# Scores as one float32 matmul each, a fused row maximum, a transposed copy of x as an input, and a new placement of the steps

## The chip, the core and the metric

The program runs on one core of one Trainium2 chip. The metric is the device time of one execution in microseconds (us). The core has five engines that run side by side, each with its own instruction queue in program order: TensorE (PE in the profile, its weight loads PEld), VectorE (DVE), ScalarE (ACT), GpSimd (POOL) and SyncE (SP), which issues nearly all DMAs. They meet through semaphores.

## What is computed

Two identical decoder layers (own weights) over 256 tokens of width 1024, all in float32:

```
xn = RMSNorm(x);  h = xn @ W_in            # 2956 columns for the four mixers
A: stick-breaking attention, strictly causal: z = q.k*scale, log-sigmoids, reverse cumulative sum, exp, @ v
B: softmax(q1 k1) - lambda * softmax(q2 k2), causal, heads of 2 x 32, RMSNorm of q, k and of the output
C: causal softmax attention (block-sparse; with 256 tokens every row sees its own block alone)
D: gated sum of three branches: 15 compressed keys; selected keys; window keys (own K and V each)
merged = sum_i sigmoid(xn @ Wg_i + b_i) * (o_i @ Wb_i)
x = x + merged @ W_out
x = x + (silu(y @ W1) * (y @ W3)) @ W2     # y = RMSNorm(x), hidden width 2816
```

There are 4 heads of 64; the tolerance calls for float32-like results.

## The kernel before, in words

**Weights by chunks.** All weights of a layer are cut into `NCH` chunks (list `CHUNKS`): each is 256 rows by up to 512 columns, 512 KB. For chunk `n` SP loads `w_raw` (a ring of 4), ACT rounds it into `w_hi` (L874, type fp32r, which PE takes in one pass), DVE puts the rest into `w_lo` (L1092), and PE (`products`, L609) makes 12 products of 512 columns: hi x hi, hi x lo and lo x hi, for two row tiles and two row blocks. ACT and DVE work `LEAD` = 2 chunks ahead of PE. The activations that meet the weights are split into hi and lo in the same way (`xt`, `ot`, `ht`).

**Steps between the chunks.** Everything else is a list of small steps. The table `PLAN` gives each step the chunk number `u` ahead of which it stands, and `RANK` its order within one `u`; every engine walks through the same lists and does its own part of each step. ACT and DVE do steps of rank under 3 before their split of chunk `u + 2`, the others after it. PE does all steps of `u` first and then the 12 products of `u`. Below, "at 38" means ahead of chunk 38. Steps that matter here:

- `x0` to `x3` (`pair`, L665): four transposes of x by PE into the PSUM tile `att`, then hi (ACT, L894) and lo (DVE, L1102).
- `Aq`, `Ak`, ... `Dk` (`qk`, L688): transposes of queries and keys. ACT copies them to `qk_hi` (L910), DVE makes `qk_lo` (L1180, L1183).
- `z` and `sm` (`causal`, L702): the scores of a pair of heads (or of the two maps of B): for each causal half of the rows hi x hi, hi x lo, lo x hi, each for both heads, which lie on different rows of PE (64 rows each, 32 in B) and go to the banks S0 and S1. `A` has 2 such steps a layer, B 4, C 2, D 4: 24 in the program, 12 matmuls each.
- DVE's part of `sm` (L1231) adds the mask and takes the row maximum; L1236 scales and negates it; ACT makes the exponentials (L930); DVE's `p` (L1248 to L1253, L1257 to L1265) scales them. `pt` (L743) transposes them in 3 pieces, ACT copies these to `ptb` (L996), and `pv` (L768; L759 in B) multiplies with v. L768 is true float32: its two halves lie on different columns of PE.
- `kct`, `cs`, `cp`, `cpt`, `cpv`: the compressed branch of D. `cs` (L839, L841) makes its scores in 16 small matmuls into S0 and S1, and DVE adds mask and low part from there (L1303, L1307).
- `o0` to `o3`: the outputs of the mixers into `ot`; `o1` is transposed by PE (L665 from `osb`).

A step that writes a bank of `att` waits for the last reader of that bank (`bank_free`): TP for transposes, S0 and S1 for scores, OB for `pv`.

Of the kernel before, what the change touches and what calls it, by code (L numbers as in the profile page):

```python
# [7 lines left out]
ALU = mybir.AluOpType  # L8
# [57 lines left out]
WARM_UP = 6, 7  # L66
RAW, WR, LEAD = 4, 4, 2


def in_cols(g):  # L70
# [9 lines left out]
    "stats": 3, "lambda": 18, "x": (0, 0, 1, 2), "f": (-2, -1, 1, 2), "m": (-1, -1, 2, 3), "h": 6,  # L80
    "sig": (50, 54, 56, 58), "o": (20, 43, 43, 58), "subln": 35, "prep": (13, 19, 27), "ngate": 27, "Aq": 6,
    "Ak": 7, "Az": (8, 14), "Asp": (11, 16), "Acum": (13, 19), "Apv": (14, 20), "Bq": 19, "Bk": 20,
    "Bsm": (21, 24, 27, 28), "Bp": (21, 24, 27, 29), "Bpt": (23, 27, 29, 32), "Bpv": (27, 29, 31, 33), "Bo": 33,
# [3 lines left out]
    "Dpt": (42, 43, 44, 45, 50, 51, 52, 54), "Dpv": (45, 53, 53, 55),  # L87
# [23 lines left out]
def maps_of(mixer, n):  # L111
# [11 lines left out]
    "x0": 0, "f0": 0, "m0": 0, "proj": 3, "zg": 4.5, "merge": 0.5, "xadd": 2.5, "act": 5, "Acum": 3.5, "Dp": 2,  # L123
    "cpv": 4, "sig": 3, "Cpv": 0.5, "cbuild": 1.5, "kct": 0.5, "x": 0.5, "Asp": 6, "Bpv": 3.5, "ck": 0.5,
    "cv": 4.5, "cs": 3.5, "prep": 1, "Csm": 4, "Dpv": 1, "lambda": 1, "stats": 1, "subln": 4.5, "Bsm": 4.5,
    "Bpt": 5.5, "ngate": 2, "Cp": 6, "h": 3, "kcprep": 1.5, "f": 4, "Bp": 4.5,
# [68 lines left out]
def steps_at(l, u):  # L195


    early = [("pair", ("x", kp)) for kp in range(2)]
    if u == NCH:
        return [(l, s) for s in STEPS[u]] if l == DEPTH - 1 else []  # L200
    todo = [(l, s) for s in STEPS[u] if not (l and s in early)]
# [14 lines left out]
class Events:  # L216


    def __init__(self, sem, order):
        self.sem, self.order, self.count = sem, order, 0  # L220
        self.place = {k: n for n, k in enumerate(order)}

    def at(self, layer, key):

        return layer * len(self.order) + self.place[key] + 1
# [71 lines left out]
def trunk_kernel(nc, x, w_in, w_gate, w_branch, w_out, w_ffn_gate, w_ffn_up, w_ffn_down,  # L297
                 norm_g, gains, lam, cmp_pe, cmp_w, b_gate, const, masks, out):
    with ExitStack() as ctx:
# [6 lines left out]
        def place(name, shape, dt, at=None):  # L306
# [20 lines left out]
        end_big = top[0]  # L327
        squares = place("squares", [P, NT, NC], F32, at=zg_at)
# [15 lines left out]
        qk_hi = [place(f"qk_hi{i}", [P, 4, SEQ], F32R) for i in range(2)]  # L344
        qk_lo = [place(f"qk_lo{i}", [P, 4, SEQ], F32R, at=zg_at + 4 * D_MODEL * (4 * i + 3)) for i in range(2)]
        kc_hl = place("kc_hl", [P, 2, 16], F32R)
# [37 lines left out]
        stat = [sm(104 + 4 * i, 4) for i in range(2)]  # L384
# [25 lines left out]
        s_ident = sem("identity_landed")  # L410
# [4 lines left out]
        s_x = [sem(f"x_quarter_landed{kp}") for kp in range(KT // 2)]  # L415
# [16 lines left out]
        att_done = Events(sem("att_done"), att_keys)  # L432
# [3 lines left out]
        hi_done = Events(sem("hi_done"), [s for s in keys("pair", "qk", "kct") if s[1] != "Dc"])  # L436
# [5 lines left out]
            "lambda", "prep", "ngate", "kcprep", "subln", "cbuild", "sm", "p", "sp", "cp")])  # L442
# [58 lines left out]
        def _(sp):  # L501
# [8 lines left out]
            def load_x(kp):  # L510
                cols = slice(2 * kp * P, (2 * kp + 2) * P)
                sp.dma_start(xs[:, :, cols], x[0, :, cols].rearrange("(t p) d -> p t d", p=P)).then_inc(s_x[kp], 16)


            load_x(0)
            sp.dma_start(ident, const[:, C_ID:C_ID + P]).then_inc(s_ident, 16)
            for k, landed in enumerate((s_half, s_raw[0])):
                sp.dma_start(w_raw[:, 0, k, :], w_in[0, k * P:(k + 1) * P, 0:NC]).then_inc(landed, 16)
            load_x(1)
            load_chunk(1)  # L520
            load_x(2)
            load_chunk(2)
            load_x(3)
# [43 lines left out]
        def _(pe):  # L567
# [10 lines left out]
            def products(l, u):  # L578
# [33 lines left out]
                if n < DEPTH * NCH - 1:  # L612
# [10 lines left out]
                    if n == 0:  # L623
                        pair(0, ("pair", ("x", 1)))
# [15 lines left out]
            def pair(l, step):  # L640
# [3 lines left out]
                if what == "x":  # L644
                    if l:
                        pe.wait_ge(dve_acc.sem, dve_acc.at(l - 1, ("xadd", ("down", kp // 2))))
                    else:
                        pe.wait_ge(s_ident, 16)
                        pe.wait_ge(s_x[kp], 16)
# [18 lines left out]
            def qk(l, step):  # L668
# [3 lines left out]
                if name[0] == "A":  # L672
                    pe.wait_ge(proj_out.sem, proj_out.at(l, ("proj", 0)))
                elif name == "Dc":
# [16 lines left out]
            def causal(buf, maps, swap=False):  # L691
# [5 lines left out]
                at = 0  # L697
                for t, (c0, c1) in enumerate((first, second)):
                    for a_, b_ in ((qk_hi, qk_hi), (qk_hi, qk_lo), (qk_lo, qk_hi)):
                        for i, (r, q, k) in enumerate(maps):  # L700
                            still, move = (k, q) if swap else (q, k)
                            mm = pe.matmul(att[:, S0 + i, at:at + c1 - c0], a_[buf][r, still, t * P:(t + 1) * P],  # L702
                                           b_[buf][r, move, c0:c1], start=not swap and t == 0 and a_ is b_,
                                           stop=t == 1 and a_ is qk_lo,
                                           skip_group_check=True)
                    at += c1 - c0
                return mm

            def scores(l, step):
# [3 lines left out]
                if n == 0:  # L713
                    pe.wait_ge(read_dve.sem, read_dve.at(l, ("qk", mixer + "k")))
# [77 lines left out]
            warm_up(WARM_UP[0])  # L792
            for l in range(DEPTH):
                for u in range(NCH):
                    for ll, step in steps_at(l, u):
                        kind, a = step
                        if kind == "pair":
                            if own_transpose(step) and (ll or step != ("pair", ("x", 1))):
                                pair(ll, step)
                            if step == ("pair", ("x", 0)) and ll == 0:  # L800
                                warm_up(WARM_UP[1])
# [29 lines left out]
                        elif kind == "cs":  # L831
                            bank_free(l, step)
                            pe.wait_ge(read_dve.sem, read_dve.at(l, ("kct", None)))
# [691 lines left out]
```

## Time and profile before

| | before |
|---|---|
| three runs, median (lowest to highest) | 870.63 us (869.18 to 871.32) |
| the profiled execution, own time | 872.5 us |
| its span, first to last instruction | 870.6 us |
| PE, DVE, ACT, POOL busy in it | 858.9, 550.9, 469.0, 159.0 us |
| granted clock of PE, mean | 0.996 |

The profile is one execution. Its own time lies 1.9 us above the span. In its rows, "start, us, engine line, out<-in" stand for groups of like instructions; a matmul's length includes its pipeline, so the time that PE spends on one is read from start to next start. The rows used are in the section after the next.

### The profile page before, as it was taken

The numbers are of one execution on the slowest core, as the hardware profiler recorded it, in microseconds if no ns is written. First come the engines' busy times: TensorE is split into PE (matmuls) and PEld (weight loads), VectorE is DVE, ScalarE is ACT, GpSimd is POOL, SyncE is SP. The second block draws the span as 40 slices with busy tenths as digits, with TensorE's granted clock in tenths as the row PEclk, the third lists the DMA queues.
The fourth block names the chain that finished last, engine by engine and source line by source line (L and its number), as shares of the span: only waits on it lengthen the run. The fifth ranks groups of instructions, "written<-read, shape, count | busy, mean of one in ns | idle before, by whom it ended". The sixth has DMA issues, their size and how long they took to land.

```text
span 870.6 us, 11639 instructions
## 1 busy us (share of the span) xinstructions
PE 858.9 (99%) x4371; PEld 700.5 (80%) x4371; DVE 550.9 (63%) x862; ACT 469.0 (54%) x721; POOL 159.0 (18%) x165
## 2 busy tenths in 40 slices
PE   8999999999999999999999999999999999999998
PEld 6888887788888888888888888777788888888886
DVE  6557877657966555555555678766588655555552
ACT  6676654556455444543457775456654744445431
POOL 0076652002500000000000858500043000000000
PEclk9999999999999999999999999999999999999999
DMA  8745453454557655555576454543545566655552
GB/s 299 242 136 184 150 195 122 145 169 146 178 161 240 178 186 180 184 192 173 172 225 209 144 174 164 185 135 110 176 162 193 175 201 184 190 180 184 194 193 73
DMA packets 103751, 154.17 MB, mean 177 GB/s; under 512 B 6800, under 2 KB 55440, under 8 KB 103440
## 3 DMA queue, kind: packets, MB, share of 16 engines
q1 hardware_dynamic: 103552, 153.42, 54.6%
q8 instruction: 35, 0.57, 0.3%
q14 instruction: 20, 0.16, 0.1%
q10 hardware_dynamic: 144, 0.01, 0.0%
HBM read 152.35 MB, written 1.05 MB: 176 GB/s over the span
## 4 chain that ended last, share of the span: by engine, by line
PE 96%; DVE 1%; ACT 1%; DMA 1%; issue 0%; SPq 0%; ACTq 0%
PE acc L609 86%; PE att L702 2%; PE att L665 2%; PE att L743 1%; PE att L768 1%; PE att L688 1%; ACT eb L930 1%; PE att L759 1%; DMA w_raw<-in_w_in 1%; DVE eb L1231 1%; PE att L727 0%; ACT ptb L996 0%; PE att L781 0%; ACT w_hi L874 0%; DVE eb L1253 0%
## 5 line engine op out<-in xcount | busy, mean ns | idle before, releaser
L1092 DVE TENSOR_TENSOR w_lo<-w_raw,w_hi 128x1024 fp32r<-128x1024 f32 (+1 forms) x276 | 342.4, 1250 | 154.5 <-ACT w_hi L874 150.1
L874 ACT ACTIVATE w_hi<-w_raw 128x1024 fp32r<-128x1024 f32 (+1 forms) x275 | 286.6, 1050 | 127.9 <-PE acc L609 123.7
L609 PE MATMUL acc<-w_hi,xt_hi 128*128 128x512 f32 (+1 forms) x864 | 243.0, 403 | 1.0 <-ACT w_hi L871 0.8
L609 PE MATMUL acc<-w_hi,xt_lo 128*128 128x512 f32 (+1 forms) x864 | 232.2, 391 | 0.0
L609 PE MATMUL acc<-w_lo,xt_hi 128*128 128x512 f32 (+1 forms) x864 | 230.3, 388 | 0.0
L609 PEld LDWEIGHTS acc<-w_hi,xt_lo 128*128 128x128 f32 x864 | 163.1, 189 | 35.2 <-DVE xt_lo L1102 0.5
L609 PEld LDWEIGHTS acc<-w_lo,xt_hi 128*128 128x128 f32 x864 | 162.4, 188 | 33.4
L609 PEld LDWEIGHTS acc<-w_hi,xt_hi 128*128 128x128 f32 x864 | 154.7, 189 | 30.3 <-ACT w_hi L871 1.2
L1357 POOL TENSOR_SCALAR small<-small 128x2 f32<-128x2 f32 (+4 forms) x14 | 7.5, 535 | 367.7 <-ACT sq_dump L968 264.2
L930 ACT ACTIVATE eb<-eb,small 128x128 f32<-128x128 f32 x80 | 35.5, 444 | 49.6 <-DVE small L1236 49.6
L1450 POOL TENSOR_TENSOR merged<-merged,prod 128x1024 f32<-128x1024 f32 x10 | 32.4, 3241 | 159.1 <-DVE prod L1141 158.3
L609 PE MATMUL acc<-w_hi,ht_hi 128*128 128x512 f32 x176 | 47.9, 391 | 0.0
L609 PE MATMUL acc<-w_hi,ht_lo 128*128 128x512 f32 x176 | 47.6, 389 | 0.0
L609 PE MATMUL acc<-w_lo,ht_hi 128*128 128x512 f32 x176 | 47.5, 389 | 0.0
L609 PEld LDWEIGHTS acc<-w_hi,ht_lo 128*128 128x128 f32 x176 | 33.0, 188 | 6.9
L609 PEld LDWEIGHTS acc<-w_lo,ht_hi 128*128 128x128 f32 x176 | 33.0, 188 | 6.9
L896 ACT ACTIVATE ht_hi<-att 128x512 fp32r<-128x512 f32 x22 | 13.2, 599 | 46.2 <-PE att L665 46.2
L609 PEld LDWEIGHTS acc<-w_hi,ht_hi 128*128 128x128 f32 x176 | 32.7, 188 | 6.6
L955 ACT ACTIVATE silu<-acc,small 128x256 f32<-128x256 f32 x44 | 18.5, 471 | 33.2 <-PE acc L609 33.2
L1169 DVE SCALAR_TENSOR_TENSOR hid<-acc,small,silu 128x256 f32<-128x256 f32 x44 | 19.3, 479 | 27.0 <-ACT silu L955 27.0
L1106 DVE TENSOR_TENSOR ht_lo<-att,ht_hi 128x512 fp32r<-128x512 f32 x22 | 15.2, 692 | 32.4 <-ACT ht_hi L896 32.4
L1231 DVE CUSTOM_DVE_ANT_0 eb<-att,cst 128x128 f32<-128x128 f32 x80 | 23.8, 353 | 12.1 <-PE att L702 11.8
(174 smaller groups left out, 774.1 us busy)
## 6 DMA issues: line engine op xcount, KB each, us to landing
w_raw<-in_w_gate SPq DMA_DIRECT2D x64, 512.0 KB, 3.6
w_raw<-in_w_ffn_gate SPq DMA_DIRECT2D x88, 256.0 KB, 2.9
w_raw<-in_w_ffn_up SPq DMA_DIRECT2D x88, 256.0 KB, 3.2
w_raw<-in_w_ffn_down SPq DMA_DIRECT2D x44, 512.0 KB, 3.5
w_raw<-in_w_in SPq DMA_DIRECT2D x39, 512.0 KB, 4.5
w_raw<-in_w_branch SPq DMA_DIRECT2D x16, 512.0 KB, 4.0
w_raw<-in_w_out SPq DMA_DIRECT2D x16, 512.0 KB, 3.5
bg<-in_b_gate SPq DMA_DIRECT2D x8, 512.0 KB, 5.3
```

Of the source, the lines that this page charges most:

```text
L609: return pe.matmul(acc[bank0 + t][:, 0:N], x_part[:, k0 + k, t * P:(t + 1) * P], w_part[:, k, 0:N], start=first, stop=last)
L665: mm = pe.transpose(att[:, b, (2 * k + t) * P:(2 * k + t + 1) * P], src, ident)
L702: mm = pe.matmul(att[:, S0 + i, at:at + c1 - c0], a_[buf][r, still, t * P:(t + 1) * P], b_[buf][r, move, c0:c1], start=not swap and t == 0 ...
L874: act.activation(w_hi[:, n % WR, :, 0:N], w_raw[:, n % RAW, :, 0:N], copy).then_inc(s_hi, 1)
L896: ins = act.activation(dst[:, 2 * kp:2 * kp + 2, :].rearrange("p k t -> p (k t)"), att[:, b, :], copy)
L930: ins = act.activation(eb[:, e, cols], eb[:, e, cols], ACT.Exp, scale=scale, bias=nbias[r][:, j:j + 1], accum_out=sums[r][:, j:j + 1])
L955: ins = act.activation(silu[:, t, :], acc[bank_pair(l, step) + t][:, 0:FC], ACT.Silu, scale=xr["f"][:, t:t + 1])
L1092: dve.tensor_tensor(w_lo[:, n % WR, :, 0:N], w_raw[:, n % RAW, :, 0:N], w_hi[:, n % WR, :, 0:N].bitcast(F32), ALU.subtract).then_inc(s_lo, 1)
L1106: ins = dve.tensor_tensor(lo[:, 2 * kp:2 * kp + 2, :].rearrange("p k t -> p (k t)"), att[:, b, :], hi[:, 2 * kp:2 * kp + 2, :].rearrange(" ...
L1169: ins = dve.scalar_tensor_tensor(out=hid[:, a % 2, t, :], in0=acc[bank_pair(l, step) + t][:, FC:2 * FC], scalar=xr["f"][:, t:t + 1], in1=s ...
L1231: ins = dve.tensor_tensor_reduce(out=eb[:, e, cols], in0=att[:, S0 + i, cols], in1=causal_add[:, P - t * P:], scale=1.0, scalar=NEG, op0=A ...
L1450: pool.tensor_tensor(merged[:, :, cols], merged[:, :, cols], prod[:, :, half_], ALU.add).then_inc(pool_done.now(step), 1)
```

## The change

- Scores: `qk_hi` and `qk_lo` become one float32 tile `qkt`, and each score block is 4 float32 matmuls instead of 12 of type fp32r. DVE's `qk` step goes, and so does its half of `kct`. The 256-column half now comes first in all mixers. `cs` becomes 8 float32 matmuls, and DVE adds no low part.
- Row maximum: L1231 now also multiplies by minus the scale and takes the minimum, straight into `nbias`; L1236 goes. In B's `p` the reciprocal that the next operation needs is issued first.
- The host also passes x transposed (`x_t`). In layer 0 the four `x` steps read it from SBUF (`xt_raw`) without PE. `xs` is loaded later, in two halves, and the constants in one DMA one chunk earlier; half of the first weight chunk is issued by ACT's queue.
- `PLAN` and `RANK` have new numbers throughout.

```diff
-WARM_UP = 6, 7
+WARM_UP = 12
...
-    "Ak": 7, "Az": (8, 14), "Asp": (11, 16), "Acum": (13, 19), "Apv": (14, 20), "Bq": 19, "Bk": 20,
+    "Ak": 7, "Az": (9, 14), "Asp": (9, 14), "Acum": (13, 17), "Apv": (16, 22), "Bq": 19, "Bk": 20,
...
-    by_dve = kind in ("pair", "sm", "cs", "cv", "cr", "kct") or (kind == "qk" and a != "Dc") or kind == "o"
+    by_dve = kind in ("pair", "sm", "cs", "cv", "cr", "o")
...
+            def load_xt(kp):
+                sp.dma_start(xt_raw[:, 2 * kp:2 * kp + 2, :], x_t[:, 2 * kp:2 * kp + 2, :]).then_inc(s_xt[kp], 16)
+            load_xt(0)
+            sp.dma_start(w_raw[:, 0, 1, :], w_in[0, P:2 * P, 0:NC]).then_inc(s_raw[0], 16)
+            load_xt(1)
             load_chunk(1)
...
-                    if u == 5 and l == 0:
-                        sp.dma_start(cst[:, C_ID + P:], const[:, C_ID + P:]).then_inc(s_const, 16)
+                    if u in (3, 4) and l == 0:
+                        c, cols = u - 3, slice((u - 3) * NC, (u - 2) * NC)
+                        sp.dma_start(xs[:, :, cols], x[0, :, cols].rearrange("(t p) d -> p t d", p=P)
+                                     ).then_inc(s_x[c], 16)
+                    if u == 4 and l == 0:
+                        sp.dma_start(cst[:, :], const).then_inc(s_const, 16)
...
-                    if n == 0:
-                        pair(0, ("pair", ("x", 1)))
...
-                at = 0
-                for t, (c0, c1) in enumerate((first, second)):
-                    for a_, b_ in ((qk_hi, qk_hi), (qk_hi, qk_lo), (qk_lo, qk_hi)):
-                        for i, (r, q, k) in enumerate(maps):
-                            still, move = (k, q) if swap else (q, k)
-                            mm = pe.matmul(att[:, S0 + i, at:at + c1 - c0], a_[buf][r, still, t * P:(t + 1) * P],
-                                           b_[buf][r, move, c0:c1], start=not swap and t == 0 and a_ is b_,
...
+                areas = ((0, first, 0), (1, second, 2 * P)) if swap else ((1, second, P), (0, first, 0))
+                for n, (t, (c0, c1), at) in enumerate(areas):
+                    for i, (r, q, k) in enumerate(maps):
+                        still, move = (k, q) if swap else (q, k)
+                        mm = pe.matmul(att[:, S0 + i, at:at + c1 - c0], qkt[buf][r, still, t * P:(t + 1) * P],
+                                       qkt[buf][r, move, c0:c1], start=not swap and n == 0, stop=n == 1,
...
-                                    pe.matmul(att[:, S0 + h % 2, at:at + 32], qk_hi[1][q],
-                                              kc_hl[r, :, :], start=True, stop=False)
-                                    mm = pe.matmul(att[:, S0 + h % 2, at:at + 16], qk_lo[1][q],
-                                                   kc_hl[r, 0, :], start=False, stop=True)
+                                    mm = pe.matmul(att[:, S0 + h % 2, at:at + 16], qkt[1][q], kct[r, :],
+                                                   start=True, stop=True)
...
+                        part = att[:, b, k * SEQ:(k + 1) * SEQ] if l or what == "f" else xt_raw[:, 2 * kp + k, :]
+                        ins = act.activation(dst[:, 2 * kp + k, :], part, copy, scale=g)
...
+            act.dma_start(w_raw[:, 0, 0, :], w_in[0, 0:P, 0:NC]).then_inc(s_half, 16)
...
-                                                           in1=causal_add[:, P - t * P:], scale=1.0, scalar=NEG, op0=ALU.add,
-                                                           op1=ALU.max, accum_out=stat[r][:, j:j + 1])
+                                                           in1=causal_add[:, P - t * P:], scale=-(DD if mixer == "B" else HD) ** -0.5,
+                                                           scalar=-NEG, op0=ALU.add, op1=ALU.min,
+                                                           accum_out=nbias[r][:, j:j + 1])
                     ins.then_inc(read_dve.now(step), 1)
-                    dve.wait_ge(read_dve.sem, read_dve.at(l, step))
-                    dve.tensor_scalar(nbias[r][:, :], stat[r][:, :],
```

**Three places on PE where steps moved.** The rows are PE's program; each run of three `acc` rows is one chunk. First, the compressed branch: before, the end of `cs` (at 38) with C's second score block (`qk_71` and `qk_73` are A's and C's tiles) right behind it, in the same banks.

```order
L839 MATMUL att<-kc_hl,qk_hi_72 128x32
L841 MATMUL att<-kc_hl,qk_lo_74 128x16
L702 MATMUL att<-qk_hi_71 128x128 x2
L702 MATMUL att<-qk_lo_73,qk_hi_71 128x128 x2
L702 MATMUL att<-qk_hi_71,qk_lo_73 128x128 x2
L702 MATMUL att<-qk_hi_71 128x256 x2
L702 MATMUL att<-qk_lo_73,qk_hi_71 128x256 x2
L702 MATMUL att<-qk_hi_71,qk_lo_73 128x256 x2
```

After, PE from `Dk` at 38 on: `cs` (at 39, 8 matmuls) is followed by a transpose of C's probabilities, which uses bank TP.

```order
L690 MATMUL att<-cst,kdup 128x128 x4
L615 MATMUL acc<-w_hi,xt_hi 128x512 x4
L615 MATMUL acc<-w_hi,xt_lo 128x512 x4
L615 MATMUL acc<-w_lo,xt_hi 128x512 x4
L836 MATMUL att<-kct,qkt_73 128x16 x8
L742 MATMUL att<-cst,eb 128x128 x3
```

C's second score block has moved to 36, two chunks and more ahead of `cs`. Second, the first softmax of B: before, PE between B's first score block (at 21) and the transpose of its probabilities (at 23).

```order
L702 MATMUL att<-qk_hi_72,qk_lo_74 128x256 x2
L609 MATMUL acc<-w_hi,xt_hi 128x396 x4
L609 MATMUL acc<-w_hi,xt_lo 128x396 x4
L609 MATMUL acc<-w_lo,xt_hi 128x396 x4
L609 MATMUL acc<-w_hi,xt_hi 128x396 x4
L609 MATMUL acc<-w_hi,xt_lo 128x396 x4
L609 MATMUL acc<-w_lo,xt_hi 128x396 x4
L743 MATMUL att<-cst,eb 128x128 x3
```

After, the same stretch of PE:

```order
L703 MATMUL att<-qkt_73 128x256 x2
L703 MATMUL att<-qkt_73 128x128 x2
L615 MATMUL acc<-w_hi,xt_hi 128x396 x4
L615 MATMUL acc<-w_hi,xt_lo 128x396 x4
L615 MATMUL acc<-w_lo,xt_hi 128x396 x4
L767 MATMUL att<-ptb,proj 64x256 x2
L767 MATMUL att<-ptb,proj 64x128 x2
L615 MATMUL acc<-w_hi,xt_hi 128x396 x4
L615 MATMUL acc<-w_hi,xt_lo 128x396 x4
L615 MATMUL acc<-w_lo,xt_hi 128x396 x4
L742 MATMUL att<-cst,eb 128x128 x3
```

A's second `pv` (at 22, before at 20) now stands between the two. Third, PE at 43: before, C's second `pv`, a transpose of D's probabilities and the transposes of `osb` (step `o1`), the last two in bank TP.

```order
L768 MATMUL att<-ptb,proj 64x256 x2
L768 MATMUL att<-ptb,proj 64x128 x2
L743 MATMUL att<-cst,eb 128x128 x3
L665 MATMUL att<-cst,osb 128x128 x4
L609 MATMUL acc<-w_hi,xt_hi 128x512 x4
```

After, PE from 43 to the start of 44:

```order
L767 MATMUL att<-ptb,proj 64x256 x2
L767 MATMUL att<-ptb,proj 64x128 x2
L767 MATMUL att<-ptb,proj 64x256 x2
L767 MATMUL att<-ptb,proj 64x128 x2
L742 MATMUL att<-cst,eb 128x128 x3
L615 MATMUL acc<-w_hi,xt_hi 128x512 x4
L615 MATMUL acc<-w_hi,xt_lo 128x512 x4
L615 MATMUL acc<-w_lo,xt_hi 128x512 x4
L665 MATMUL att<-cst,osb 128x128 x4
```

Both `pv` of C are together now, and a whole chunk lies between the two uses of TP.

## Rows read from the trace of the kernel before

**Rows 1.** Page: PE busy in the span; the chain that ended last, by line.

```profile
PE 858.9 (99%) x4371; PEld 700.5 (80%) x4371; DVE 550.9 (63%) x862; ACT 469.0 (54%) x721; POOL 159.0 (18%) x165
PE acc L609 86%; PE att L702 2%; PE att L665 2%; PE att L743 1%; PE att L768 1%; PE att L688 1%; ACT eb L930 1%; PE att L759 1%; DMA w_raw<-in_w_in 1%; DVE eb L1231 1%; PE att L727 0%; ACT ptb L996 0%; PE att L781 0%; ACT w_hi L874 0%; DVE eb L1253 0%
```

**Rows 2.** Timeline of PE, layer 0, at 51: start us, length us, engine, line.

```profile
187.84 0.49 PE L743 MATMUL att<-cst,eb 128*128 128x128 f32 x3
188.08 1.18 PE L609 MATMUL acc<-w_hi,xt_hi 128*128 128x512 f32 x4
189.10 1.08 PE L609 MATMUL acc<-w_hi,xt_lo 128*128 128x512 f32 x4
190.01 1.07 PE L609 MATMUL acc<-w_lo,xt_hi 128*128 128x512 f32 x4
```

**Rows 3.** Waits of PE over the span: waiting line <- releaser: us, times, longest.

```profile
PE att L702 <- DVE csc L1307: 1.9, 2, 0.9
PE att L743 <- DVE eb L1253: 1.8, 2, 0.9
...
PE att L665 <- ACT ptb L996: 1.2, 2, 0.6
```

**Rows 4.** Timeline of PE: `pv` and `z` at 14, then B's first scores.

```profile
50.91 0.87 PE L768 MATMUL att<-ptb,proj 128*64 128x256 f32 x8
51.72 0.39 PE L694 MATMUL att<-cst 128*128 128x256 bf16 x2
52.04 0.39 PE L702 MATMUL att<-qk_hi 64*128 64x256 f32 x2
...
52.88 1.19 PE L609 MATMUL acc<-w_hi,xt_hi 128*128 128x512 f32 x4
...
74.57 0.33 PE L702 MATMUL att<-qk_hi 32*128 32x128 f32 x2
...
75.46 0.81 PE L609 MATMUL acc<-w_hi,xt_hi 128*128 128x396 f32 x3
```

**Rows 5.** Timeline of PE at 38: C's second scores behind `cs`, chunk 38.

```profile
136.29 0.33 PE L702 MATMUL att<-qk_hi 64*128 64x128 f32 x2 [0.93 <-DVE csc L1307]
...
137.18 2.07 PE L609 MATMUL acc<-w_hi,xt_hi 128*128 128x512 f32 x4
```

**Rows 6.** Stretches: busy PE, PEld, DVE, ACT, POOL; then PE's granted clock, DMA share, GB/s.

```profile
10.00:15.00 5.00, 4.97 (x26) 3.77 (x26) 4.62 (x7) 3.89 (x8) 0.00 (x0) 1.00 1.05 379
...
133.80:137.20 3.40, 2.47 (x32) 1.92 (x30) 2.45 (x8) 0.31 (x1) 1.75 (x2) 1.00 0.71 204
137.20:140.60 3.40, 3.40 (x10) 2.75 (x9) 2.68 (x15) 1.88 (x9) 0.00 (x0) 0.50 0.31 108
...
567.30:570.70 3.40, 3.40 (x9) 2.63 (x8) 2.71 (x17) 2.18 (x9) 0.00 (x0) 0.50 0.23 87
```

**Rows 7.** Timeline, DVE: the scaling in B's first softmax (at 21).

```profile
76.80 0.64 DVE L1236 TENSOR_SCALAR small<-small 128x4 f32<-128x4 f32 x1
```

**Rows 8.** Timeline from the start: chunk 1, x2's transposes, chunk 1, `stats`, chunks 3, 5, 6.

```profile
9.15 1.06 ACT L874 ACTIVATE w_hi<-w_raw 128x1024 fp32r<-128x1024 f32 x1 [1.32 <-DMA w_raw<-in_w_in]
...
10.75 0.60 PE L665 MATMUL att<-cst,xs 128*128 128x128 f32 x4
...
11.10 1.18 PE L609 MATMUL acc<-w_hi,xt_hi 128*128 128x512 f32 x4
...
16.59 1.05 ACT L968 ACTIVATE sq_dump<-xs 128x1024 f32<-128x1024 f32 x1
...
17.46 1.07 PE L609 MATMUL acc<-w_hi,xt_hi 128*128 128x512 f32 x4
...
18.66 2.00 ACT L874 ACTIVATE w_hi<-w_raw 128x1024 fp32r<-128x1024 f32 x2
```

**Rows 9.** Timeline of PE at 43 (first two) and at 53 (last).

```profile
159.33 0.55 PE L743 MATMUL att<-cst,eb 128*128 128x128 f32 x3
160.46 0.33 PE L665 MATMUL att<-cst,osb 128*128 128x128 f32 x1 [0.58 <-ACT ptb L996]
...
194.10 1.52 PE L768 MATMUL att<-ptb,proj 128*64 128x256 f32 x16
```

More of the change, by code:

```diff
@@ L122 @@
 RANK = {
[L123 to L126, printed above, removed]
+    "x0": 0, "f0": 0, "m0": 0, "proj": 4, "zg": 4.5, "merge": 0.5, "xadd": 0.5, "act": 4.5, "Acum": 5.5,
+    "Dp": 6, "cpv": 6, "sig": 4.5, "Cpv": 3, "cbuild": 1.5, "kct": 4.5, "x": 0.5, "Asp": 6, "Bpv": 4.5, "ck": 1,
+    "cv": 1.5, "cs": 3.5, "prep": 0.5, "Csm": 3, "Dpv": 4.5, "lambda": 2.5, "stats": 1.5, "subln": 6, "Bsm": 4,
+    "Bpt": 6, "ngate": 1.5, "Cp": 5, "h": 5, "kcprep": 2, "f": 4, "Bp": 5.5,
 }
@@ L200, in steps_at @@
         return [(l, s) for s in STEPS[u]] if l == DEPTH - 1 else []
-    todo = [(l, s) for s in STEPS[u] if not (l and s in early)]
+    now = STEPS[u]
+    if l == 0:
+        late = ("stats", "x")
+        now = sorted([s for s in now if s != late] + [late] * (u == STATS_0), key=rank)
+    todo = [(l, s) for s in now if not (l and s in early)]
     if l and u == 0:
@@ L216, with __init__ @@
 class Events:
-    def __init__(self, sem, order):
-        self.sem, self.order, self.count = sem, order, 0
+    def __init__(self, sem, order, absent=0):
+        self.sem, self.order, self.count, self.absent = sem, order, absent, absent
         self.place = {k: n for n, k in enumerate(order)}
     def at(self, layer, key):
-        return layer * len(self.order) + self.place[key] + 1
+        return layer * len(self.order) + self.place[key] + 1 - self.absent
     def now(self, key):
@@ L327, in trunk_kernel @@
         end_big = top[0]
+        xt_raw = place("xt_raw", [P, KT, SEQ], F32, at=zg_at + 16 * D_MODEL)
         squares = place("squares", [P, NT, NC], F32, at=zg_at)
@@ L341, in trunk_kernel @@
         hid = place("hid", [P, 2, NT, FC], F32, at=big2 + 4 * NT * FC)
-        qk_hi = [place(f"qk_hi{i}", [P, 4, SEQ], F32R) for i in range(2)]
-        qk_lo = [place(f"qk_lo{i}", [P, 4, SEQ], F32R, at=zg_at + 4 * D_MODEL * (4 * i + 3)) for i in range(2)]
-        kc_hl = place("kc_hl", [P, 2, 16], F32R)
+        qkt = [place(f"qkt{i}", [P, 4, SEQ], F32) for i in range(2)]
+        kct = place("kct", [P, 16], F32)
         kcvt = place("kcvt", [P, 2, SEQ], F32)
@@ L414, in trunk_kernel @@
         s_gt = sem("norm_gains_landed")
-        s_x = [sem(f"x_quarter_landed{kp}") for kp in range(KT // 2)]
+        s_x = [sem(f"x_half_landed{c}") for c in range(2)]
+        s_xt = [sem(f"xt_quarter_landed{kp}") for kp in range(KT // 2)]
         s_raw = [sem(f"raw_landed{i}") for i in range(RAW)]
@@ L508, in load_chunk @@
                                  ).then_inc(s_raw[n % RAW], 16)
[L510 to L519, printed above, removed]
+            def load_xt(kp):
[3 more added lines that the diff above has]
+            load_xt(1)
             load_chunk(1)
-            load_x(2)
+            load_xt(2)
             load_chunk(2)
-            load_x(3)
+            load_xt(3)
             for l in range(DEPTH):
@@ L877, in pair_hi @@
                 (what, kp), b = step[1], banks_of(step)[0]
-                if own_transpose(step):
+                if what == "x" and l == 0:
+                    act.wait_ge(s_xt[kp], 16)
+                elif own_transpose(step):
                     act.wait_ge(att_done.sem, att_done.at(l, step))
@@ L1101, in pair_lo @@
                         g = gt[:, 2 * kp + k + (KT if what == "f" else 0):][:, 0:1]
-                        ins = dve.scalar_tensor_tensor(out=lo[:, 2 * kp + k, :], in0=att[:, b, k * SEQ:(k + 1) * SEQ],
-                                                       scalar=g, in1=hi[:, 2 * kp + k, :].bitcast(F32),
-                                                       op0=ALU.mult, op1=ALU.subtract)
+                        part = att[:, b, k * SEQ:(k + 1) * SEQ] if l or what == "f" else xt_raw[:, 2 * kp + k, :]
+                        ins = dve.scalar_tensor_tensor(out=lo[:, 2 * kp + k, :], in0=part, scalar=g, in1=hi[:, 2 * kp + k, :].bitcast(F32), op0=ALU.mult,
+                                                       op1=ALU.subtract)
                 else:
@@ L1304, in do @@
                                                 .to_broadcast([P, 2, 2, 16]), ALU.add)
-                    settled(ins)
-                    for t in range(NT):
-                        ins = dve.tensor_tensor(hv[:, t], sc[:, t, :, :, 16:32], hv[:, t], ALU.add)
                     ins.then_inc(read_dve.now(step), 1)
```

78 lines of the change are left out of this document (28 added, 50 removed), and 6 rows, old and new, of the table PLAN.

## The prediction, as it was put on record

> **What bounds the kernel now.** I read the page first: PE is busy 99% of the span, and the chain that ended last is PE's own products for 86% of it [rows 1]. So nothing on another engine costs time unless PE stops for it, and the questions are what PE spends between products, and where it waits. The timeline of PE gives the cadence: four products of 512 columns start 0.91 us after the four before them (189.10 to 190.01, [rows 2]), 0.227 us each, in every undisturbed chunk. 86% of 870.6 us is 749 us; the change leaves these products alone. The rest, some 120 us, is the start, the small steps between chunks, the waits and a slower clock. The list of PE's waits is short: 1.9, 1.8 and 1.2 us in three lines, twice each, once in each layer [rows 3]. Last I looked for the stretches in which the granted clock is not 1: it is 0.50 (1.2 instead of 2.4 GHz) from 137.2 to 140.6 and again from 567.3 to 570.7 [rows 6]. Ahead of the first, PE had made the 16 tiny matmuls of `cs` and stood still for 0.93 us [rows 5]; it was busy 2.47 of 3.40 us [rows 6].
>
> **Term 1, the score blocks.** A block of `z` takes 0.84 us (52.04 to 52.88), one of B 0.89 (74.57 to 75.46) [rows 4]; the one of C behind the wait also 0.88 (136.29 to 137.18, [rows 5]). 20 of the 24 blocks are of the second kind. It has 384 columns in three passes, two heads side by side: 1152 columns, at 0.227 us per 512 only 0.51 us. The other 0.35 is weight loads and the passage into and out of the divided array. The new block is not in the trace, but a near relative is: `pv` at L768 is true float32, divided by columns instead of rows, two halves of 256 + 128 columns, and takes 0.81 us (50.91 to 51.72, [rows 4]). Four passes of 384 columns are 1536 columns or 0.68 us, so there the passage costs 0.13. I take 0.80: 20 x 0.08 + 4 x 0.04 = **1.8 us less**. Bounds: 0.75 a block (3 us less), as the last 128-column pass may hide part of the passage, and 0.68 + 0.35 = 1.03 (3.9 us more). Here the row says that a fourth pass is nearly free, since a block was not held by its columns. The Trainium skill ("FP8 and Floating Point Precision", TensorE Precision Notes) counts "True FP32: 4 passes through PE array", a rule against trading three passes for one such matmul: by it alone a block grows by 0.17 us and the term is 4 us more; that is rival 2. `cs` keeps 16 small matmuls in the records (8 float32 ones, two records each, as L768 shows: 8 for 4), so I cost it at nothing; bound: 0.2 us either way.
>
> **Term 2, `cs` apart from C's scores.** Before, the scores at 38 wait 0.93 us for DVE to empty S0 and S1 [rows 5]. Now a transpose in TP follows, and the next user of S0 and S1 is D's first block, at 40, behind a whole chunk of 2.7 us. DVE needs some 1 us for the read, and is at most its own split away. So 0.93 us goes in each layer. With it goes, I expect, the slow clock: 3.4 us at half clock cost 1.7 us, in each layer. Together 2 x 2.6 = **5.3 us less**. What the clock wants is not in the rows; the new stretch at 39 has the same small matmuls but no stop, so PE does 0.9 us more of products in it. If the clock still falls there, 3.4 us come back.
>
> **Term 3, B's first softmax.** PE waits 0.9 us at 23 in each layer for DVE's `p` [rows 3]. The chain is scores, DVE maximum, L1236, ACT exponentials, DVE `p`, PE. L1236 goes, and ACT starts 0.64 us sooner, its length there [rows 7]; and A's second `pv`, 0.81 us, now stands at 22 between the two [rows 4]. Against it: these 0.81 us stood ahead of the scores before, so the scores come earlier and may find DVE still at its split of chunk 23, which costs the chain up to 0.6. 0.64 + 0.81 - 0.6 is still about 0.9: **1.8 us less**; bound 0.9.
>
> **Term 4, PE at 42 to 46.** At 43 the three transposes start at 159.33 and those of `osb` only at 160.46, 1.13 us later, since ACT must first read TP [rows 9]; three transposes by themselves take 0.24 (187.84 to 188.08, [rows 2]) and some 0.06 more ahead of other small work. Moved to 44 this wait is gone: 0.8 a layer. The two `pv` of C next to each other cost 1.52 - 0.87 = 0.65 us for the second [rows 4, 9] instead of 0.81 plus its own passage in and out (about 0.2): 0.35. Some steps stand alone now and pay 0.1 each for the first product behind them (188.08 to 189.10 is 1.02 instead of 0.91, [rows 2]): I charge 0.05. 2 x 1.1 = **2.2 us less**, bounds 1 and 3. The wait between the two transposes at 42 stays.
>
> **Term 5, the rest of the table.** `z` and `pv` at 14, `cum` and `Bq` at 19, `Bk` and `pv` at 20 part: 3 x 0.07 more a layer. At 27, 31 and 55 steps are regrouped: 0.3 less. **0.2 us less** over both layers; bound 1 us either way. The feed-forward steps (`h`) move by one chunk and keep their cost, since PE never waited for them. Everything that ACT and DVE no longer do is hidden under PE's 99%.
>
> **Term 6, the start.** The transposes of x1, x2 and x3 lie between products, 0.35 us (10.75 to 11.10, [rows 8]) + 0.1 each, together 1.3 us. But the start is paced by the DMAs: ACT waits 1.32 us for the raw chunk 1 [rows 8], and then still copies x1. Up to that chunk the new order loads 64 KB less (no identity), 0.2 us at 379 GB/s [rows 6]. From chunk 2 on PE has its data in time. So the removal of x3's and part of x2's transposes counts, 0.6, plus 0.2: **0.8 us less**; bounds 0 and 1.3. New on SP's queue, ahead of chunk 5, are the two halves of `xs` and all constants, 1.5 MB more than stood there: 4.1 us at 379 GB/s [rows 6]. `stats` waits for them on ACT with the split of chunk 5 queued behind it. ACT took chunks 5 and 6 at 18.66 without a wait [rows 8]; PE will want chunk 5 at 16.7 + 2 x 2.7 = 22.1. If it had landed only just before 18.66, it now comes at 22.8 and PE waits 1.8 us; ACT had been at the squarings of `stats` from 16.59 on [rows 8], so it may as well have landed at 16.5 and come at 20.6. I take nothing, and 1.8 for the range.
>
> **Sum:** 1.8 + 5.3 + 1.8 + 2.2 + 0.2 + 0.8 = 12.1 us. Against the profiled execution's own 872.5 us this is 860.4; against the median of the runs, 1.9 us lower, **858.5 us** (1.4% faster). About 0.3% (2.6 us) can be told from no change, so "faster" means under 868.0 and "slower" over 873.2.
>
> **Rivals.**
> (1) *The two heads of a block do not run side by side.* The mechanism on the other side: float32 on divided rows is in no row, only on divided columns. If the second head waits for the first, a block is 2 x 0.68 + 0.13 = 1.49 us, 0.69 more than forecast, 24 times: 16.5 us more, **875 us**. It decides from 0.6 us a block. Against it: fp32r on divided rows and float32 on divided columns both run in pairs in [rows 4] (L768's two halves, 1536 columns each, would take 1.36 us one after the other, not 0.81). The Trainium skill ("TensorEngine Tiling (Array Packing)", Key Properties) says that different tiles "can execute LdWeights and Matmul in parallel", without a word on types; by it this rival falls. Chance 0.06.
> (2) *The fourth pass is paid in full*: 1.03 us a block, 5.7 us more than forecast, **864.2 us**. For it: the 0.35 us of passage and loads are the same instructions. Against it: L768. Chance 0.15.
> (3) *A wait takes the place of those removed*: S0 and S1 at 36 or 40, TP at 44, or the clock falls once in each layer for another reason. Each is 0.5 to 0.9 us a layer, the clock 1.7; two of these in both layers give 3 to 5 us: **862.5 us**. For it: DVE has both C blocks, `zg`, `o` and `p` within two chunks at 35 and 36. Chance 0.17.
> (4) *The start gives the gain back*: PE has less to do than before while it waits for chunks 0 and 1, so the clock may be halved once (1.7), or chunk 5 is late (1.8), or both: **861 us**. Chance 0.12.
> (5) *The gains are larger*: the block is at its lower bound and ends other short waits: **856 us**. Chance 0.08.
> The forecast itself has the remaining 0.42, from 857 to 860.5.
>
> **How the numbers follow.** Rivals 2 to 5 all end under 868, so faster has 0.42 + 0.15 + 0.17 + 0.12 + 0.08 = 0.94, less 0.02 for two of them at once with a size missed: 0.92. Rival 1 ends at 875 and, with a shorter wait of the second head, within the band: slower 0.05, same 0.03. The range takes the forecast and most of rivals 2 to 5: 855.5 to 864.5 us.
>
> **What would show it.** In the changed kernel: score blocks of 0.80 us from first start to the next product (1.03: rival 2; 1.5: rival 1); no idle time of PE at `cs` and granted clock 1.00 in every stretch of both layers; no line "`eb` <- DVE" among PE's waits; `osb`'s transposes behind products without a stop; chunk 1's first product near 10.9 us and chunk 3's near 16.7 instead of 17.46 [rows 8]. Each term can be read by itself. The forecast fails if PE's waits sum to more than 3 us past the start, or if the clock is at 0.50 anywhere past 5 us.

## The result, and the profile after

| | before | after |
|---|---|---|
| runs, median (lowest to highest) | 870.71 us (869.18 to 871.32) | 861.99 us (861.62 to 862.15) |
| profiled execution, own time | 872.5 us | 862.15 us |
| its span | 870.6 us | 860.3 us |
| granted clock of PE, mean | 0.996 | 1.000 |

The changed kernel is 1.0% faster: the ratio of the times is 0.9897, 95% interval 0.9883 to 0.9911. The forecast was 858.5 us with a range of 855.5 to 864.5: the sign and the range held, the middle was 3.5 us too low. Between the two profiled executions the fall is 10.35 us, between the medians 8.7; that difference is a finding of its own (below).

The profile after reads like that of before [rows 1], with PE's products now at 88% of the chain. Busy times on the page:

```profile
PE 853.6 (99%) x4258; PEld 694.7 (81%) x4258; DVE 538.1 (63%) x820; ACT 474.8 (55%) x725; POOL 158.4 (18%) x165
```

PE's waits in it (waiting line, releaser: us, times, longest), against [rows 3]:

```profile
PE att L788 <- DVE warm L1109: 1.2, 1, 1.2
PE att L742 <- ACT ptb L993: 1.2, 2, 0.6
PE acc L615 <- ACT w_hi L863: 0.8, 1, 0.8
```

The waits for `csc`, for `eb` and of `osb`'s transposes are gone. What is left is the wait between the two transposes at 42, which the prediction had left in place, and two at the start, which the kernel before has too. The wait at 42 stood in the list of before as a fourth line, of the same size:

```profile
PE att L743 <- ACT ptb L996: 1.2, 2, 0.6
```

The stretches that had run at half clock [rows 6], read again in the changed kernel (us, busy PE, PEld, DVE, ACT, POOL, then the clock, DMA share, GB/s):

```profile
137.20:140.60 3.40, 3.40 (x19) 2.69 (x19) 2.82 (x9) 2.03 (x4) 2.73 (x4) 1.00 0.63 226
567.30:570.70 3.40, 3.40 (x18) 2.76 (x17) 3.30 (x13) 2.48 (x9) 0.00 (x0) 1.00 0.48 154
```

Twice as many matmuls in the same 3.4 us, at full clock. The timeline of PE after, at B's first scores and through 23, against [rows 4]:

```profile
72.44 0.92 PE L703 MATMUL att<-qkt 32*128 32x256 f32 x8
73.30 0.99 PE L615 MATMUL acc<-w_hi,xt_hi 128*128 128x396 f32 x4
...
75.68 0.87 PE L767 MATMUL att<-ptb,proj 128*64 128x256 f32 x8
76.48 0.99 PE L615 MATMUL acc<-w_hi,xt_hi 128*128 128x396 f32 x4
...
78.75 0.49 PE L742 MATMUL att<-cst,eb 128*128 128x128 f32 x3
```

The block takes 73.30 - 72.44 = 0.86 us by these rows; over all 24 blocks it is 0.851 to 0.855, where the forecast had 0.80. A's `pv` stands at 75.68, and the transposes at 78.75 start without a wait. `z` takes as long (49.70 to 50.55), against 0.84 before.

### The profile page after: what moved, and what is told of

Read it like the earlier page. It is cut to its first block, busy times and chain, and to the rows that moved or that the text cites. A ratio compares the mean times of both kernels' runs of the same rounds, so it can differ in the third digit from the quotient of the medians.

```text
span 860.3 us, 11371 instructions
## 1 busy us (share of the span) xinstructions
PE 853.6 (99%) x4258; PEld 694.7 (81%) x4258; DVE 538.1 (63%) x820; ACT 474.8 (55%) x725; POOL 158.4 (18%) x165
## 4 chain that ended last, share of the span: by engine, by line
PE 99%; DMA 1%; ACT 0%; DVE 0%; issue 0%; ACTq 0%
PE acc L615 88%; PE att L703 2%; PE att L665 2%; PE att L767 1%; PE att L742 1%; PE att L690 1%; PE att L758 1%; DMA w_raw<-in_w_in 1%; PE att L726 0%; PE att L780 0%; PE att L836 0%; PE att L845 0%; ACT ptb L993 0%; PE att L727 0%; PE att L696 0%; PE att L815 0%
## 5 line engine op out<-in xcount | busy, mean ns | idle before, releaser
L1337 POOL TENSOR_SCALAR small<-small 128x2 f32<-128x2 f32 (+4 forms) x14 | 9.9, 706 | 360.9 <-ACT sq_dump L965 265.0
L1338 POOL TENSOR_TENSOR small<-small 128x2 f32<-128x2 f32 (+4 forms) x14 | 33.4, 2388 | 1.2
```

Source lines behind the costliest of these rows:

```text
L1338: return pool.tensor_tensor(dst, dst, exps_, ALU.pow)
```

## The experiments

### What the scatter of the kernel before is made of

The kernel before was run again unchanged.

> The kernel before, unchanged, three more times, to see what its own scatter is made of. Its runs lie between 869.18 and 872.5 us, those of the changed kernel within 0.53 us. Theory A: the half clock behind `cs` comes in some executions and not in others, once for each layer, and costs 1.7 us each time; then the mean granted clock of a run and its time go together: 0.996 with about 872.5 us (both layers), 0.998 with about 870.8 (one), 1.000 with about 869.1 (none). Theory B: it comes in every execution, as in the profiled one, and the scatter is something else; then all runs show 0.996 whatever their time.

Each run's mean granted clock is known beside its time. With the runs of the kernel before that stood beside the other experiments there are 44:

| mean clock | runs | time, median (lowest to highest) |
|---|---|---|
| 0.996 | 22 | 872.3 us (872.02 to 873.13) |
| 0.998 | 21 | 870.8 us (870.16 to 871.40) |
| 1.000 | 1 | 869.54 us |

Theory A fits, and the groups do not overlap: the half-clock stretch comes 0, 1 or 2 times in an execution. Between the two large groups it costs 1.5 us, and 1.3 us down to the single run at 1.000, somewhat less than the 1.7 expected. So the profiled execution with its two stretches was one kind of run, and the median of three another. (The unprofiled runs of the main comparison have no clock on record; by their times, 869.18 to 871.32 us, none of them is of the slowest group.) The medians of before in the four comparisons, 870.7 to 872.1 us, tell how many of each kind were drawn. Where small differences count, the runs below are therefore set against 872.3 us, or against runs of the same clock.

### Term 2 alone, each half of the change alone

```diff
-Csm (35, 38), cs 38, cp 38
+Csm (35, 36), cs 39, cp 39
```

> The kernel before with one edit: C's second score block at 36 instead of 38, and `cs` with `cp` at 39 instead of 38, as the change has it. Term 2 alone. Theory A of the prediction: the wait of 0.93 us goes in both layers and the clock stays at 1.00; against the profiled 872.5 us that is 1.9 + 3.4 = 5.3 less, 867.2 us; if the half clock was only there in some executions, the fall of the medians is 1.9 + 1.7 = 3.6 us, to 867.1, all the same, and the scatter of the runs falls under 0.6 us. Rival: `cs` and its small neighbours bring the half clock at 39 just as well; then only the wait goes, the time is 868.8 on the median and still scatters over 2 to 3 us.

Measured: 867.98 us (867.43 to 868.46), all five runs at a clock of 0.999 or 1.000; 4.3 us under the 0.996 group, 4.9 between the profiled executions (872.5 to 867.64). That is 0.8 us more than expected, and the runs scatter over 1.0 us instead of under 0.6. The rival is out all the same: none of the five runs had the half clock, although the 16 small matmuls are still there and only PE's stop behind them is gone. In the 3.4 us around `cs`, against [rows 6]:

```profile
136.50:139.90 3.40, 3.40 (x29) 2.74 (x28) 3.36 (x8) 0.74 (x1) 0.00 (x0) 1.00 0.61 184
```

`cs` fills 137.75 to 138.77 there, 1.02 us. In the changed kernel it takes as much: the float32 form costs nothing, as forecast. Next, the tables on the kernel before:

```diff
-PLAN, RANK of before
+PLAN, RANK of after        # nothing else
```

> The kernel before with the tables PLAN and RANK of the changed one and nothing else: scores in three passes with low parts by DVE, L1236 in place, x transposed by PE. Theory: the table is worth what terms 2, 4 and 5 say (5.3 + 2.2 + 0.2 less one half-clock stretch on the median, 1.7) and the part of term 3 that the moved `pv` brings (0.3 in each layer, the wait does not go, since L1236 still stands in the chain): 6.6 us, 864.1 us. Rival: the table needs the lighter DVE; the DVE halves of the `qk` steps (0.6 us each) and L1236 make new waits of PE at 21 to 24, 36 and 40 to 46, and the kernel ends at 866 to 868 us.

Measured: 867.60 us (867.26 to 868.06), clock 1.000. The rival was right: the tables bring 4.7 us against 872.3, of which the clock is most, and PE has new waits. The two lines for `qk_lo` stand in neither kernel:

```profile
PE att L743 <- ACT ptb L996: 1.8, 4, 0.7
...
PE att L688 <- DVE qk_lo L1183: 0.9, 2, 0.5
PE att L743 <- DVE qk_lo L1183: 0.8, 2, 0.4
...
PE att L743 <- DVE eb L1253: 0.2, 1, 0.2
```

One of these stops stands right behind the same 16 small matmuls, 0.40 us long, and the clock stays at 1.00 around it:

```profile
139.52 0.55 PE L743 MATMUL att<-cst,eb 128*128 128x128 f32 x3 [0.40 <-DVE qk_lo L1183]
...
137.20:140.60 3.40, 3.00 (x27) 2.36 (x26) 3.40 (x5) 0.00 (x0) 3.32 (x2) 1.00 0.49 152
```

And the other way round, the changed code with the old tables:

```diff
-PLAN, RANK of after
+PLAN, RANK of before       # nothing else
```

> The changed kernel with the tables PLAN and RANK of the kernel before: float32 scores, fused maximum and x passed transposed, without a step moved. Theory from the trace of the changed kernel: 0.6 us for the blocks (0.853 us each instead of 0.885), 1.3 for L1236 ahead of B's first `p`, 1.5 for the start and some 0.4 for the shorter DVE part of `cs`: 3.8 us less than before, 866.9 us on the median, and the half clock behind `cs` is still there, because C's scores still wait in its banks, so the runs scatter over 1.7 us or more. Rival: the half clock belonged to the 16 small matmuls of two kinds and goes with them: 865 us and a scatter under 0.6 us.

Measured: 866.08 us, four runs of 865.86, 865.89, 866.27 and 868.66; the last has a clock of 0.997, the others 1.000. PE still stops behind `cs`, but for 0.55 instead of 0.93 us, since DVE has less to do there:

```profile
131.77 1.09 PE L836 MATMUL att<-kct,qkt 64*128 64x16 f32 x16
133.40 0.92 PE L703 MATMUL att<-qkt 64*128 64x256 f32 x8 [0.55 <-DVE csc L1286]
134.25 1.21 PE L615 MATMUL acc<-w_hi,xt_hi 128*128 128x512 f32 x4
```

So here the slow stretch mostly stays away. The fourth run has no trace; that the half clock is what made it some 2.7 us longer is read from its clock of 0.997 alone. Neither theory had that. Two things differ from the kernel before at this place, the length of the stop and the small matmuls (8 of float32 instead of 16 of fp32r), and this run does not part them. The kernel with the new tables alone does so in part: with the old matmuls and a stop of 0.40 us, none of its four runs had the half clock. That speaks for the stop's length, without a run that changes the length alone. The waits of this run also price the code's share in B's first softmax:

```profile
PE att L703 <- DVE csc L1286: 1.1, 2, 0.5
PE att L742 <- DVE eb L1236: 1.1, 2, 0.5
```

B's first wait falls from 0.9 to 0.55 us in each layer, not by the 0.64 of [rows 7]. The traces show where the rest went. Between DVE's maximum and ACT's first exponential there were 0.72 us before and there are 0.04 now, so the whole 0.64 is saved there. But DVE's last step of `p`, the scaling, takes 0.3 us longer (first row before, second row this run; why it does is not shown):

```profile
79.90 0.89 DVE L1253 SCALAR_TENSOR_TENSOR eb<-eb,small 128x128 f32<-128x128 f32 x2
...
77.16 1.23 DVE L1236 SCALAR_TENSOR_TENSOR eb<-eb,small 128x128 f32<-128x128 f32 x2
```

The 0.64 itself was a rare length: 18 of the 20 rows of the old L1236 take 0.17 us, and only the two in B's first softmax 0.62 and 0.64. In the kernel with the new tables alone it takes 0.18 there, and the wait is 0.1 on the mean (0.2, once). So the tables alone take away 0.8 of the 0.9 us, the code alone 0.35, and in the changed kernel the two overlap.

The two halves against 872.3: tables alone 4.7, code alone 6.2, both 10.3 to 10.6. Without the two half-clock stretches (3.4 us by term 2's working; the tables remove them, the code mostly) that is 1.3, 2.8 and 7.1: together they bring 3 us more than the sum of both alone (2.3 if the two stretches cost only the 2.8 us that the groups of runs show). Most of it is in the waits: with the tables alone PE has 2.5 us of waits more than in the changed kernel (0.6 for `ptb`, 1.7 for `qk_lo`, 0.2 for `eb`).

### Type or order of the halves

The diff changed two things in a score block: the type, and which half comes first.

```diff
-for t in (0, 1):           # 128 columns, then 256; three fp32r passes each
+for t in (1, 0):           # 256 columns first
```

> The kernel before with the half of 256 columns ahead of the half of 128 in the 20 score blocks of B, C and D (in A's `z` it stands first already), still three fp32r passes. The forecast gave the whole gain of a block to the type. Theory A: what a block gained (0.885 us before, 0.853 after) came from the order of the halves, and float32 for itself costs time: then these 20 blocks take 0.84 us as `z` does, 20 x 0.044 = 0.9 us less, and executions with the clock at 0.996 take 871.5 us instead of 872.4. Theory B: `z` is shorter for another reason (the mask matmul ahead of it) and the order is worth nothing: blocks of 0.885 us, 872.4 us at a clock of 0.996.

```profile
74.67 0.38 PE L702 MATMUL att<-qk_hi 32*128 32x256 f32 x2
...
75.51 0.80 PE L609 MATMUL acc<-w_hi,xt_hi 128*128 128x396 f32 x3
```

Blocks of 0.831 to 0.847 us, mostly 0.836, instead of 0.885. Runs with a clock of 0.998 take 869.8 us instead of 870.8, with 0.996 871.3 instead of 872.3: 1.0 us less at equal clock, by the order alone. Two of the ten runs had a clock of 1.000 (868.0 us both), where the kernel before had one of 44, though the stop behind `cs` is as long as before. The profiled execution, at 0.998, has the half clock in one layer and not in the other, after the same work of PE:

```profile
133.80:137.20 3.40, 2.47 (x32) 1.98 (x31) 2.39 (x8) 0.31 (x1) 1.66 (x1) 1.00 0.73 206
137.20:140.60 3.40, 3.40 (x10) 2.68 (x11) 2.75 (x16) 1.99 (x9) 0.00 (x0) 0.59 0.31 105
563.90:567.30 3.40, 2.47 (x30) 2.20 (x29) 2.40 (x14) 0.31 (x1) 0.91 (x1) 1.00 0.82 281
567.30:570.70 3.40, 3.40 (x18) 2.81 (x17) 2.71 (x15) 2.75 (x10) 0.00 (x0) 1.00 0.04 16
```

So a stop of 0.93 us brings the half clock in some executions and places and not in others; what decides between them is open. The fourth corner:

```diff
-areas = ... else ((1, second, P), (0, first, 0))
+areas = ... else ((0, first, 0), (1, second, P))      # float32, 128 columns first
```

> The changed kernel with the half of 128 columns first again in the score blocks of B, C and D, float32. The other corner of the same square. Theory A (the order counts for both types): these 20 blocks take 0.853 + 0.044 = 0.90 us, 0.9 us more in all, 862.9 us. Theory B (the order is worth nothing, the type gives the gain): 0.853 us and 862.0 us.

```profile
72.16 0.92 PE L703 MATMUL att<-qkt 32*128 32x128 f32 x8
73.01 0.99 PE L615 MATMUL acc<-w_hi,xt_hi 128*128 128x396 f32 x4
```

0.854 to 0.857 us a block and 861.66 us (861.44 to 861.78): no loss. Theory A holds for three passes, theory B for float32:

| us a block | 128 first | 256 first |
|---|---|---|
| fp32r, 12 matmuls | 0.885 | 0.836 |
| float32, 4 matmuls | 0.855 | 0.853 |

Float32 gains 0.03 on the old order and loses 0.017 to the better order of the old type. On PE it is worth nothing; what it brings is on DVE and ACT.

### Do the two heads run side by side

```diff
-for i, (r, q, k) in enumerate(maps):
+for i, (_, q, k) in enumerate(maps):
+    r = maps[0][0]
```

> The changed kernel with both matmuls of each pair in the score blocks on the rows of the first head (the second head's scores are left out, the first's made twice), so that the two can't run beside each other. It measures rival 1 of the prediction. If the pairs of the changed kernel do run side by side, a block grows from 0.853 us to twice its columns: 2 x 1536 columns at 0.227 us per 512 are 1.36, with the passage of 0.13 to 0.17 some 1.5 us, 24 x 0.65 = 15.6 us more, 877.6 us. If they never ran side by side, the block stays at 0.85 and the kernel at 862.0 us.

```profile
73.30 1.57 PE L704 MATMUL att<-qkt 32*128 32x256 f32 x8
74.80 0.45 PE L615 MATMUL acc<-w_hi,xt_hi 128*128 128x396 f32 x1
```

73.30 to 74.80: all 24 blocks take 1.499 to 1.503 us, the kernel 877.13 us (one run). That is rival 1 to 0.01 us in the block and 2 us in the time: 15.5 us is what running side by side is worth here, and the changed kernel has it for float32 on divided rows.

### Twenty nanoseconds behind side work

```diff
-kct = place("kct", [P, 16], F32)
+kct = place("kct", [P, 32], F32)      # the second half is not used
```

> The changed kernel with 64 bytes a partition more for the tile `kct`, so that all tiles placed behind it have the addresses of the kernel before. Behind side work, a chunk's 12 products take 2.622 us from first to last start in the changed kernel, 2.602 in the kernel before, over 50 such chunks, 1.1 us in all, and the same program text does it with the old tables too. Theory A: it is the addresses in SBUF; then these chunks take 2.602 us again and the kernel 861.0 us. Theory B: it is something in PE's own stream (its instructions, 8 fewer in each score block, stand elsewhere in memory): 2.622 us and 862.0 us.

The same `h` step and chunk in the changed kernel and, in the second fence, in the padded one:

```profile
265.38 0.60 PE L665 MATMUL att<-cst,hid 128*128 128x128 f32 x4
265.73 1.18 PE L615 MATMUL acc<-w_hi,xt_hi 128*128 128x512 f32 x4
...
268.58 0.62 PE L615 MATMUL acc<-w_hi,xt_hi 128*128 128x512 f32 x2
```

```profile
265.33 0.60 PE L665 MATMUL att<-cst,hid 128*128 128x128 f32 x4
265.69 1.17 PE L615 MATMUL acc<-w_hi,xt_hi 128*128 128x512 f32 x4
...
268.52 0.84 PE L615 MATMUL acc<-w_hi,xt_hi 128*128 128x512 f32 x3
```

From chunk to chunk 2.85 and 2.83 us; from first to last product start 2.622 and 2.602, the latter as in the kernel before. Theory A holds: the chunks of the padded kernel take the kernel before's times one by one, odd ones of 2.628 among them. The time is 861.05 us (861.00 to 861.63), 0.6 to 0.9 under the changed kernel's two medians (861.66 and 861.99); the 120 or so chunks behind side work add up to 0.6 us less. Which of the moved tiles it is, and why an address matters only behind side work, was not tried.

### The wait that was left

```diff
-Cpt (39, 40, 42, 42), Cpv (43, 43), o (22, 44, 44, 58)
+Cpt (39, 40, 42, 43), Cpv (44, 44), o (22, 46, 44, 58)
-Dsm (40, 42, ..), Dp (41, 42, ..), Dpt (43, ..)
+Dsm (40, 43, ..), Dp (41, 43, ..), Dpt (44, ..)
```

> The changed kernel unchanged, on the same chip as the next two, as their base: 862.0 us, all runs within 0.6 us and at a mean clock of 0.999 to 1.000, whatever the runs of the kernel before beside it show. If the half clock can still come in it, one run would stand 1.7 us or more above the others at a lower clock.

> The changed kernel with C's fourth transpose at 43 instead of 42, so that a chunk lies between it and the third, which uses the same bank; behind it C's two `pv` at 44, D's first transpose at 44, D's second scores at 43 and `osb`'s transposes at 46. It takes up what the prediction left in place: the wait of 0.58 us between the two transposes at 42, once in each layer. Theory: the wait goes and nothing takes its place, less 0.1 us for one more step that stands alone: 1.0 us less, 861.0 us. Rival: S0 and S1 at 43, or C's `pv` waiting for ACT's copy of the fourth transpose one chunk later, take the place of it: 862.0 us or a little more, with a new line among PE's waits.

> Both together: the 64 bytes at `kct` (861.05 us measured by itself) and C's fourth transpose at 43. Theory: the two have nothing to do with each other and add, 860.1 us. If the move of steps brings chunks that the addresses don't help, 860.5 us.

Measured: 861.66 us (861.61 to 861.76) for the base, 860.93 (860.73 to 861.49) with the step moved, 860.25 (859.97 to 860.53) with both. PE at 43 and 44 in the kernel with only the step moved:

```profile
149.16 0.49 PE L742 MATMUL att<-cst,eb 128*128 128x128 f32 x3
149.57 0.92 PE L703 MATMUL att<-qkt 64*128 64x256 f32 x8
...
153.37 1.52 PE L767 MATMUL att<-ptb,proj 128*64 128x256 f32 x16
```

The wait is gone and no other came: past the warm-up at the start, the list of PE's waits is empty. The gain is 0.7 of the 1.0 us expected, and the two edits add (1.4 us). The last kernel is the fastest of these: ratio to the kernel before 0.9871, 95% interval 0.9854 to 0.9887.

## Why the prediction was right, and where it was off

Against the profiled 872.5 us, in us less:

| term | forecast | measured | from |
|---|---|---|---|
| 1 score blocks | 1.8 | 0.6 | 20 x 0.032 less, 4 x 0.013 more |
| 2 `cs` and the clock | 5.3 | 4.9 | the edit alone, profiled executions |
| 3 B's first softmax | 1.8 | 1.8 | the wait of 0.9 is gone twice |
| 4 PE at 42 to 46 | 2.2 | 2.1 | first products of chunks 40 and 58, both layers: 2.4, less the 0.3 of term 1's blocks there |
| 5 rest of the table | 0.2 | -0.2 | starts of chunks, at 13 to 19, 27 and 31 |
| 6 start | 0.8 | 1.5 | chunk 6 at 24.48 instead of 25.98 |
| addresses of tiles | none | -0.6 to -0.9 | the padded kernel |
| sum | 12.1 | 9.8 to 10.1 | 10.35 between the profiled executions |

The rest to 10.35 lies around `cs`: from chunk 32 to chunk 40 the changed kernel gains 5.2 us over both layers without the score blocks, some 0.4 more than that edit alone.

The time lies in the range, but not for the reason that the range gave. The prediction's own case went from 857 to 860.5 us and was missed by 1.5; the range reached to 864.5 to take in rivals 2 to 4, and none of them happened. That it was wide enough for the error of term 1 and for the stretch counted twice (below) is luck.

**Term 1** failed in size, by 1.2 us. The step that failed is the near relative: `pv`, on divided columns, had shown 0.13 us for the passage, and a block on divided rows needs 0.17 (0.853 - 0.68; with both heads on the same rows 1.501 - 1.36 = 0.14). Float32 on rows is nearly held by its columns: on the same rows a block grows by 0.65 us for 0.68 us of columns. And the 0.885 of the old block was in part the order of its halves, which the prediction had in its own rows (`z` at 0.84 with 256 first, B at 0.89 with 128 first, [rows 4]) and did not ask about. The Trainium skill ("FP8 and Floating Point Precision", TensorE Precision Notes) counts four passes for true FP32; at equal order the fourth pass shows, at 0.017 us rather than the 0.17 of its columns.

**Term 2** was right in mechanism, wait and clock both, and the experiment with that edit alone brings 4.9 of 5.3 us. What failed is how it was carried over to the median. The prediction noted that the profiled execution lay 1.9 us above the median of the runs and took off the same 12.1 us from both. But those 1.9 us were one of the two half-clock stretches, which the median run had not. Its saving was counted twice: 1.7 of the 3.5 us by which the time was missed; the other 1.8 are 12.1 - 10.35. (That the median run had one such stretch less is read from its time and the groups above, since it was not traced.)

**Term 3** came out as said, for another split of the causes: the code is worth 0.35 us in B's chain, since the 0.64 of L1236 was partly lost again in a longer `p`, and the tables with the moved `pv` are worth 0.8 by themselves, where the prediction had both needed. **Term 4** came out. **Term 5** had its sign wrong by a small amount, unseen beside the rest. **Term 6** was underrated: chunk 1 starts at 9.47 us (forecast 10.9) and chunk 3 at 15.95 (forecast 16.7). The prediction had the DMA pace the start; but chunk 1's raw weights were taken by ACT at 7.47 instead of 9.15 [rows 8], 1.7 us earlier rather than 0.2:

```profile
7.47 1.06 ACT L869 ACTIVATE w_hi<-w_raw 128x1024 fp32r<-128x1024 f32 x1 [0.69 <-DMA w_raw<-in_w_in]
...
19.74 1.06 ACT L869 ACTIVATE w_hi<-w_raw 128x1024 fp32r<-128x1024 f32 x1 [0.58 <-DMA w_raw<-in_w_in]
```

Why it came so much earlier was not taken apart; in the first 5 us the DMAs moved 191 GB/s instead of 149. The second row is chunk 5: it had landed by 19.7 us, earlier than both cases of the working (20.6 and 22.8), was rounded by 20.8 and wanted at 21.4, so nothing was paid.

**The rivals.** (1) is measured and out: 1.50 us a block is what it would have been, 0.853 is what it was. The Trainium skill ("TensorEngine Tiling (Array Packing)", Key Properties) has different tiles work in parallel; for float32 on divided rows this case's traces agree, with 0.853 us against 1.501. (2) is out in size, 0.853 us a block against 1.03, though it was right that the fourth pass is not free. Its price was also added up a little high: from blocks of 0.885 and 0.84 us the 1.03 gives 3.7 us more, not 3.9. (3) took no form: no new wait in the changed kernel. It was a fair rival: with the tables alone it happens. (4) did not come: no stretch of the changed kernel's profile is at half clock past 5 us. (5) is out. The forecast's own test, "nowhere at 0.50 past 5 us" and "no line `eb` <- DVE", was met.

## What to carry to other kernels

Before a saving read in one profiled execution is taken off a median, ask whether the thing saved is in every execution: here the granted clock of each run split the times of one program into three groups 1.3 to 1.5 us apart, and the profiled run was of the slowest. When a change swaps two things in one block (a type and an order), price each; the order of the halves was worth more on PE than the type. And a table of positions is tuned to the lengths of the steps on the other engines: new tables on old code, or new code on old tables, gave 4.7 and 6.2 us, together 10.3 to 10.6.

## What the runs showed of the hardware

- A stop of PE of 0.93 us behind 16 small matmuls brought 3.4 us at half clock at 0, 1 or 2 of 2 places in an execution of the kernel before (by the mean clock, 43 of 44 executions had at least one), and with the order of the score halves swapped in 8 of 10 executions. A stop of 0.40 us behind the same matmuls brought it in none of four, no stop in none of five. A stop of 0.55 us behind 8 float32 matmuls left the clock at 1.000 in three of four executions; the fourth had 0.997.
- Three fp32r passes in row pairs take 0.836 or 0.885 us by whether the half of 256 or of 128 columns comes first; float32 takes 0.853 or 0.855.
- Moving tiles by 64 bytes a partition changed the 12 products behind most transposes from 2.622 to 2.602 or 2.606 us, and undisturbed chunks (2.493) not at all.
